# One 4 MB transfer for an expert's input matrix, where there were two of 2 MB

## The chip, the cores and the metric

The kernel runs on one core of one Trainium2 chip. TensorE is written PE, VectorE DVE, ScalarE ACT, GpSimd POOL and SyncE SP. The metric is the device time of one launch in microseconds, as the median of several runs. Before the change it is 3769.35 us (three runs, 3766.24 to 3770.93).

## What is computed

Two networks of two layers each run one behind the other on 512 tokens of width 1024, all in fp32. The first network's layer is a token mixer followed by a mixture of experts; the second's is attention, gating and convolution followed by a dense feed-forward part. The change lies in the mixture of experts of the first network. Cut to that part, the reference is:

```python
def hier_moe(h, w_rg, b_rg, w_re, b_re, w1, w2):       # w1: 32 x 1024 x 1024, w2: 32 x 512 x 1024
    t = h.reshape(-1, d_)                              # 512 tokens
    ...                                                # each token picks a group of 8 experts and 2 experts in it
    order = jnp.argsort(flat_e)
    xs = t[flat_tok[order]]
    hu = lax.ragged_dot(xs, w1, sizes)                 # each expert's tokens by its input matrix
    h_gate, h_up = jnp.split(hu, 2, axis=-1)
    ys = lax.ragged_dot(jax.nn.silu(h_gate) * h_up, w2, sizes)
    ys = ys * flat_gate[order][:, None]
    return jnp.zeros_like(t).at[tok_s].add(ys)

for l in range(DEPTH):                                 # DEPTH = 2
    x = x + g1 * token_mixer(...)
    x = x + g2 * hier_moe(...)
```

An expert's input matrix `w_expert_in[l, e]` is 1024 x 1024 fp32, 4 MB; its output matrix `w_expert_out[l, e]` is 512 x 1024, 2 MB. All 32 experts are read in each layer.

## The kernel before, in words

The program is written out engine by engine, with semaphores between them and no scheduler: each engine runs its own instructions in the order in which they stand, and a waiting instruction holds up all that stands behind it on that engine. Block A (the first network) is a hardware loop over two layers, block B (the second network) another.

**The ring.** All weights go through `ring`, six slots of 2 MB each (128 partitions x 16 KB). In block A's projections slots 0 to 2 and at times 3 to 5 are given to named blocks of weights (`blocks_a`). In the expert phase slots 0, 1, 2 belong to the even experts (u = 0) and 3, 4, 5 to the odd ones (u = 1). An expert's input matrix, cut into rows 0 to 511 and rows 512 to 1023, fills the first two of its slots (j = 0 and j = 1), its output matrix the third (j = 2). Row 128 k + p of a matrix lies in partition p, so each descriptor moves one row of 4 KB.

**SP** issues all weight transfers. `expert` (L581 on) issues those of one expert: for each j it waits until PE has finished with that slot's former contents (`m_in_read[0]`, `m_in_read[1]`, `m_down_made`) and then starts the transfer. The transfers of experts 1 and 0 of a layer are issued ahead of the phase, as soon as the last projections that used those slots are done (`layer_first`); the others come in a loop of pairs. A transfer that SP starts joins one hardware queue, which works the transfers off in order. Behind the last expert of layer 0 SP goes on with the first weights of layer 1 (`w_ada`, then `w_in`, L616), behind the last expert of layer 1 with block B's (`w_in_2`, L645).

**PE** works pair by pair (`pair`, L1219). For an expert it does `gate_up` (input matrix, two runs of 16 matmul instructions of 512 columns, one for each j, with a wait for each slot's landing semaphore), then `turn_x` (transposes of the next expert's tokens), `indices` (which tokens the expert after that takes), and `down` (transposes of the activation, then 16 matmul instructions with the output matrix). The SiLU and the product between `gate_up` and `down` are on ACT (L2245) and DVE (L1816, L1822).

**POOL** gathers an expert's token rows with an indirect transfer (L790) and scatters its results into a scratch tensor (L799). When the last scatter of a layer has landed, POOL loads the results back token by token in four steps (L726, `s_units<-ys_scratch`), DVE adds the two experts' results (L1880), PE turns them (L1237), and DVE adds them to the residual (L1887). Then the next layer, or block B, begins.

Of the kernel before, what the change touches and what calls it, by code (L numbers as in the profile page):

```python
# [35 lines left out]
D = 1024  # L36
# [279 lines left out]
def program(nc, ctx, inp, out):  # L316
    def sb(name, shape, dt=F32):
        return ctx.enter_context(nc.sbuf_tensor("s_" + name, shape, dt))

    def sem(name):  # L320
        return ctx.enter_context(nc.semaphore(name))
# [9 lines left out]
    ring = sb("ring", [P, RING, SLOT])  # L331
# [129 lines left out]
    weights_in_m = [sem(f"m_weights_slot{s}") for s in range(RING)]  # L461
# [73 lines left out]
    def settle(eng):  # L535

        eng.sem_inc(settled, 1)
# [4 lines left out]
    def slot_view(s, k, n):  # L542
        return ring[:, s, 0:k * n].rearrange("p (k n) -> p k n", k=k)
# [14 lines left out]
    def _(sp):  # L558
        def kn(w, c0, n):
            return w.rearrange("(k p) n -> p k n", p=P)[:, :, c0:c0 + n]  # L560
# [6 lines left out]
        def source_a(name, l):  # L567
            kind, j = name[0], name[1] if len(name) > 1 else 0
            if kind == "ada":
                return KD, 512, kn(inp["w_ada"][l], 512 * j, 512)  # L570
            if kind == "lr":
                return KD, 32, kn(inp["w_in"][l], C_LR, 32)
            if kind in ("ya", "yb"):
                return 4, 512, kn(inp["w_branch_a" if kind == "ya" else "w_branch_b"][l], 512 * j, 512)
            if kind == "wo":
                return KD, 512, kn(inp["w_out"][l], 512 * j, 512)
            c = {"gqk": 0, "gv": C_GV, "gg": C_GG, "dq": C_DQ, "dk": C_DK, "dv": C_DV, "ga": C_GA, "gb": C_GB}[kind]
            return KD, 512, kn(inp["w_in"][l], c + 512 * j, 512)
# [3 lines left out]
        def expert(l, number, e, u, layer_first):  # L582

            for j in range(3):
                s = 3 * u + j
                if layer_first:

                    sp.wait_ge(TA.done.sem, TA.done_at(l, RA.reader_last(s) if s < 3 else ("gb", 7)))
                    settle(sp)

                sp.wait_ge(freed_in_m[j].sem, freed_in_m[j].at(number, u - 1))
                settle(sp)
                if j < 2:
                    sp.dma_start(slot_view(s, 4, D), kn(inp["w_expert_in"][l, e], 0, D)[:, 4 * j:4 * j + 4, :]).then_inc(weights_in_m[s], 16)
                else:
                    sp.dma_start(slot_view(s, 4, D), kn(inp["w_expert_out"][l, e], 0, D)).then_inc(weights_in_m[s], 16)

        with sp.Fori(0, DEPTH) as l:
            settle(sp)
            before = sp.value_load(cells[0:1, 0:1], min_val=0, max_val=BLOCKS)  # L600
            for name, *_ in RA.blocks:
                s = RA.slot(name)
                reader = RA.reader_before(name)
                if reader is None:

                    sp.wait_ge(freed_in_m[s % 3].sem, freed_in_m[s % 3].at(before * 2, s // 3 - 1))
                else:
                    sp.wait_ge(TA.done.sem, TA.done_at(l, reader))
                settle(sp)
                if name[0] == "rt":  # L610
                    v = slot_view(s, KD, 36)
                    sp.dma_start(v[:, :, 0:4], kn(inp["w_router_group"][l], 0, 4)).then_inc(weights_in_a[s], 16)
                    sp.dma_start(v[:, :, 4:36], kn(inp["w_router_expert"][l], 0, 32)).then_inc(weights_in_a[s], 16)
                else:
                    k, n, src = source_a(name, l)
                    sp.dma_start(slot_view(s, k, n), src).then_inc(weights_in_a[s], 16)  # L616

            for u in (1, 0):
                expert(l, before * 2, u, u, True)
            sp.wait_ge(routed.sem, routed.at(l, 1))  # L620
            settle(sp)
            ahead = sp.value_load(cells[0:1, 1:2], min_val=NEXP // 2 - 1, max_val=BLOCKS // 2 - 1)

            with sp.Fori(0, ahead) as pair:
                for u in range(2):
                    e = sp.value_load(block_expert[0:1, bass.ds(2 * pair + (2 + u), 1)], min_val=0, max_val=NEXP - 1)
                    expert(l, before * 2 + (2 * pair + 2), e, u, False)

        total = sp.value_load(cells[0:1, 0:1], min_val=0, max_val=BLOCKS)
        with sp.Fori(0, DEPTH) as l:  # L630
            for name, *_ in RB.blocks:
                s = RB.slot(name)
# [9 lines left out]
                j = name[1]  # L642
# [3 lines left out]
                elif name[0] == "up":  # L646
                    i, n = UPS[j]
# [211 lines left out]
    def _(pe):  # L859
        def mm(o, lhsT, rhs, start, stop):  # L860
            return pe.matmul(o, lhsT=lhsT, rhs=rhs, start=start, stop=stop)  # L861
# [37 lines left out]
        with pe.Fori(0, DEPTH) as l:  # L899
# [183 lines left out]
            for i in range(HEADS * NT + 2):  # L1083
# [8 lines left out]
                if i >= 2:  # L1092
                    j = i - 2
# [88 lines left out]
            def gate_up(number, pairs, u):  # L1182

                for j in range(2):
                    s = 3 * u + j
                    pe.wait_ge(weights_in_m[s], pairs * 16 + 16)
                    if j == 0:
                        pe.wait_ge(m_xsT_copied.sem, m_xsT_copied.at(number, u + 1))
                        pe.wait_ge(m_act_made.sem, m_act_made.at(number, u - 1))
                    w = slot_view(s, 4, D)  # L1190
                    for k in range(4):
                        for c in range(2):
                            half = slice(CAP * c, CAP * c + CAP)
                            both = w[:, k, :].rearrange("p (h f) -> p h f", h=2)[:, :, 256 * c:256 * c + 256]
                            last = mm(psum[half, u, :].rearrange("p (h f) -> p h f", h=2), xsT[u][:, k, CAP * j:CAP * j + CAP],
                                      both, j == 0 and k == 0, j == 1 and k == 3)
                    last.then_inc(m_in_read[j].sem, m_in_read[j].more())
# [18 lines left out]
            def pair(number, pairs, e, more_come):  # L1216
                for u in range(2):
                    gate_up(number, pairs, u)
                    if more_come or u == 0:  # L1219
                        turn_x(number, pairs, u + 1)  # L1220
                    if more_come:
                        indices(number, e + (u + 2), u + 2)
                    down(number, pairs, u)
# [17 lines left out]
        with pe.Fori(0, DEPTH) as l:  # L1241
# [117 lines left out]
            for j in range(PAIRS + 3):  # L1359
# [21 lines left out]
                if j in FILL:  # L1381
                    name, a, b = FILL[j]
# [1078 lines left out]
```

## Time and profile before

| | us |
|---|---|
| median of three runs | 3769.35 |
| the profiled execution, its own time | 3768.46 |
| its span in the profile | 3766.8 |
| PE busy | 3173.7 (84% of the span) |
| DVE busy | 1138.5 (30%) |
| ACT busy | 946.6 (25%) |
| POOL busy | 807.7 (21%) |
| moved by DMA | 663.67 MB, of which the SP queue 623.43 MB |

The profile's time starts at the span's start; the 1.66 us between the profiled execution's span and its own time lie outside it. All stretches below are given in microseconds from that start. Layer 0's expert phase is at 679 to 1226 us, layer 1's at 1877 to 2448 us; block B follows. A line such as "PE L861 MATMUL ... x16" sums up 16 instructions that stand next to each other; the figure ahead of it is how long they took together, and the bracket behind it the idle time of that engine ahead of them and what ended it. Matmuls come from one helper (L861), so they are told apart by their operands: `s_ring,s_units 128*64` are those with expert weights. The durations of PE are modelled from records of which a few per cent can be missing.

### The profile page before, as it was taken

The page shows a single profiled execution, that of the slowest core. Times are in us where ns is not written, and L with a number is a line of the kernel's source. Part 1 is how long each engine was busy: PE and PEld are TensorE (multiplying, and loading weights), DVE is VectorE, ACT ScalarE, POOL GpSimd, SP SyncE. Part 2 cuts the span into 40 slices and gives each one's busy share as a digit, 9 for nine tenths or more (in the row PEclk, how much of TensorE's full clock was granted, in tenths as well). Part 3 has the DMA queues.
Part 4 walks back from the last instruction along what each step waited for, and adds up shares of the span by engine and source line. Part 5 has one row for each costly group of instructions (what it writes and reads, how often), then busy time and mean ns, then how long its engine had stood idle before and what let it go on. Part 6 is the DMA issues. An engine that isn't in the chain of part 4 may idle for free. (4 is left out here: it accounts for less than half of the span.)

```text
span 3766.8 us, 42402 instructions
## 1 busy us (share of the span) xinstructions
PE 3173.7 (84%) x15027; PEld 2050.9 (54%) x15027; DVE 1138.5 (30%) x2001; ACT 946.6 (25%) x1337; POOL 807.7 (21%) x382
## 2 busy tenths in 40 slices
PE   6985898788785797699788778597899998889999
PEld 4763564333332575365433323275688776568877
DVE  4555312211111447421311111134243303424330
ACT  4323201111110523211111111133343323334331
POOL 3311010111111222000011111231134343014432
PEclk7997898899997898799799999889899998989999
DMA  5124123799998112413299999810222231022232
GB/s 206 68 77 144 68 90 131 310 408 409 408 407 339 68 68 79 153 54 138 90 396 408 409 409 408 309 57 23 68 83 86 79 118 63 23 68 90 79 88 69
DMA packets 291822, 663.67 MB, mean 176 GB/s; under 512 B 20254, under 2 KB 114772, under 8 KB 291664
## 3 DMA queue, kind: packets, MB, share of 16 engines
q1 hardware_dynamic: 273792, 623.43, 44.6%
q0 software_dynamic: 17872, 38.14, 2.8%
q8 instruction: 98, 1.61, 0.2%
q14 instruction: 60, 0.49, 0.0%
HBM read 653.64 MB, written 25.69 MB: 180 GB/s over the span
## 5 line engine op out<-in xcount | busy, mean ns | idle before, releaser
L861 PE MATMUL psum<-s_parts 128*128 128x512 f32 (+1 forms) x3744 | 951.9, 406 | 84.0 <-ACT s_units L2050 37.7
L861 PEld LDWEIGHTS psum<-s_parts 128*128 128x128 f32 (+1 forms) x3744 | 723.1, 194 | 279.3 <-ACT s_units L2050 46.0
L861 PE MATMUL psum<-s_ring,s_units 128*64 128x512 f32 x3168 | 742.5, 617 | 135.2 <-DMA s_ring<-in_w_expert_in 96.1
L839 POOL TENSOR_TENSOR s_parts<-s_ring,s_parts 128x4096 fp32r<-128x4096 f32 (+2 forms) x52 | 407.9, 7843 | 875.4 <-ACT s_parts L2050 875.4
L861 PEld LDWEIGHTS psum<-s_ring,s_units 128*64 128x64 f32 x3168 | 247.2, 141 | 587.0 <-issue 446.8
L861 PE MATMUL psum<-s_h_low,s_parts 128*128 128x512 f32 (+1 forms) x1872 | 469.8, 391 | 11.2 <-DVE s_hid_low L2021 11.2
L861 PEld LDWEIGHTS psum<-s_h_low,s_parts 128*128 128x128 f32 (+1 forms) x1872 | 350.0, 188 | 95.1 <-DVE s_hid_low L2021 12.1
L861 PE MATMUL psum<-s_units 128*128 (+9 forms) x1520 | 303.6, 420 | 81.8 <-ACT s_units L2050 31.4
L748 POOL TENSOR_TENSOR s_parts<-s_ring,s_parts 128x4096 fp32r<-128x4096 f32 (+1 forms) x22 | 180.5, 8209 | 595.9 <-ACT s_parts L2050 595.9
L2050 ACT ACTIVATE s_parts<-s_ring 128x4096 fp32r<-128x4096 f32 (+3 forms) x74 | 237.3, 3210 | 254.6 <-PE psum L861 103.5
L861 PEld LDWEIGHTS psum<-s_units 64*128 64x128 f32 (+3 forms) x1520 | 177.8, 196 | 163.5 <-issue 109.1
L1810 DVE TENSOR_SCALAR s_put_at<-psum,s_half_row 128x1 int32<-128x1 f32 x66 | 14.4, 218 | 702.9 <-DMA ys_scratch<-s_units,s_put_at 702.9
L861 PE MATMUL psum<-s_units,s_ring 128*128 128x512 f32 x512 | 221.5, 592 | 3.3 <-DVE s_units L1694 3.3
L790 POOL DMA_INDIRECT s_units<-h_scratch,s_take_at x66 | 83.0, 1258 | 594.6 <-DVE s_take_at L1805 474.0
L2050 ACT ACTIVATE s_units<-psum 128x512 f32<-128x512 f32 (+1 forms) x252 | 145.3, 599 | 257.3 <-PE psum L861 210.1
L861 PEld LDWEIGHTS psum<-s_units,s_ring 128*128 128x128 f32 x512 | 97.1, 190 | 123.3 <-issue 122.7
L2030 DVE SCALAR_TENSOR_TENSOR s_units<-psum,s_par,s_units 128x511 f32<-128x511 f32 x88 | 66.0, 750 | 280.8 <-ACT s_units L2413 280.8
L2413 ACT ACTIVATE s_units<-psum,s_par 128x512 f32<-128x512 f32 x88 | 60.7, 690 | 308.7 <-PE psum L861 308.7
L799 POOL DMA_INDIRECT ys_scratch<-s_units,s_put_at x66 | 67.2, 1018 | 322.3 <-ACT s_units L2251 288.0
L2251 ACT ACTIVATE s_units<-psum,s_gsl 128x512 f32<-128x512 f32 x66 | 45.4, 687 | 359.2 <-PE psum L861 359.2
L1504 DVE RECIPROCAL s_temps<-s_temps 128x512 f32<-128x512 f32 x36 | 120.7, 3353 | 25.1 <-ACT s_temps L2075 25.1
L2245 ACT ACT_TABLE_LOAD x31 | 39.8, 1283 | 270.3 <-PE psum L861 270.3
(336 smaller groups left out, 2608.1 us busy)
## 6 DMA issues: line engine op xcount, KB each, us to landing
s_ring<-in_w_expert_in SPq DMA_DIRECT2D x132, 2048.0 KB, 23.9
s_ring<-in_w_expert_out SPq DMA_DIRECT2D x66, 2048.0 KB, 24.8
s_ring<-in_w_in SPq DMA_DIRECT2D x28, 2048.0 KB, 8.0
s_ring<-in_w_ada SPq DMA_DIRECT2D x24, 2048.0 KB, 8.2
s_ring<-in_ffn_w_up SPq DMA_DIRECT2D x40, 1024.0 KB, 6.6
s_ring<-in_ffn_w_down SPq DMA_DIRECT2D x16, 1408.0 KB, 7.0
s_ring<-in_w_out SPq DMA_DIRECT2D x8, 2048.0 KB, 7.8
s_units<-ys_scratch POOLq DMA_DIRECT2D x16, 512.0 KB, 6.0
```

Source lines behind the costliest of these rows:

```text
L748: pool.tensor_tensor(parts[:, s, 0:size], ring[:, s, 0:size], parts[:, 4 + n % 2, 0:size].bitcast(F32), ALU.subtract).then_inc(weights_low ...
L790: pool.indirect_dma_start(out=xs[u % 2], out_offset=None, in_=h2_dram[:, :], in_offset=bass.IndirectOffsetOnAxis(ap=take_at[:, u % 2, 0:1] ...
L799: pool.indirect_dma_start(out=ys_dram[:, :], out_offset=bass.IndirectOffsetOnAxis(ap=put_at[:, u, 0:1], axis=0), in_=ys[u], in_offset=None ...
L839: pool.tensor_tensor(parts[:, s, 0:size], ring[:, s, 0:size], parts[:, 4 + n % 2, 0:size].bitcast(F32), ALU.subtract).then_inc(weights_low ...
L861: return pe.matmul(o, lhsT=lhsT, rhs=rhs, start=start, stop=stop)
L1504: link(ve.reciprocal(T[:, 2, :], T[:, 3, :]))
L1810: ve.tensor_scalar(put_at[:, u % 2, :], psum[:, 7, 1:2], 2.0, half_row[:, 0:1], ALU.mult, ALU.add).then_inc(m_put_written.sem, m_put_writt ...
L2030: link(ve.scalar_tensor_tensor(out=up_t[:, b, 1:SEQ], in0=o[:, 0:SEQ - 1], scalar=w[0], in1=up_t[:, b, 1:SEQ], op0=ALU.mult, op1=ALU.add))
L2050: return ae.activation(o, i, ACT.Copy) if scale is None else ae.activation(o, i, ACT.Copy, scale=scale)
L2245: ae.activation(sil[u], psum[:, u, 0:256], ACT.Silu).then_inc(m_silu_made.sem, m_silu_made.more())
L2251: ae.activation(ys[u], psum[:, 5 + u, :], ACT.Copy, scale=gsl[:, u:u + 1]).then_inc(m_ys_made.sem, m_ys_made.more())
L2413: ae.activation(up_t[:, n % 4, :], o, ACT.Copy, scale=par[:, col:col + 1]).then_inc(up_centre.sem, up_centre.more())
```

## The change

SP no longer starts a transfer at j = 0; it still waits there for `m_in_read[0]`. At j = 1, after the wait for `m_in_read[1]`, it starts one transfer of the whole matrix into the two neighbouring slots, with the same 4 KB rows, and it reports on the first slot's semaphore. PE waits for that semaphore ahead of its first run of `gate_up` and no longer between the two. The output matrix's transfer, the matmuls, and the semaphores by which PE gives slots back are the same.

```diff
                 sp.wait_ge(freed_in_m[j].sem, freed_in_m[j].at(number, u - 1))
                 settle(sp)
-                if j < 2:
-                    sp.dma_start(slot_view(s, 4, D), kn(inp["w_expert_in"][l, e], 0, D)[:, 4 * j:4 * j + 4, :]).then_inc(weights_in_m[s], 16)
-                else:
+                if j == 1:
+                    both = ring[:, s - 1:s + 1, :].rearrange("p a (k n) -> p (a k) n", n=D)
+                    sp.dma_start(both, kn(inp["w_expert_in"][l, e], 0, D)).then_inc(weights_in_m[s - 1], 16)
+                elif j == 2:
                     sp.dma_start(slot_view(s, 4, D), kn(inp["w_expert_out"][l, e], 0, D)).then_inc(weights_in_m[s], 16)
...
                 for j in range(2):
                     s = 3 * u + j
-                    pe.wait_ge(weights_in_m[s], pairs * 16 + 16)
                     if j == 0:
+                        pe.wait_ge(weights_in_m[s], pairs * 16 + 16)
                         pe.wait_ge(m_xsT_copied.sem, m_xsT_copied.at(number, u + 1))
                         pe.wait_ge(m_act_made.sem, m_act_made.at(number, u - 1))
```

SP, in the loop over pairs, the transfers of the even expert of the pair. `m_in_weights_read0` and `1` count PE's two runs of `gate_up`, `m_down_made` counts `down`. Before:

```order
L594 ISA [waits m_in_weights_read0]
L594 DMA s_ring<-in_w_expert_in 128x4x1024
L594 ISA [waits m_in_weights_read1]
L594 DMA s_ring<-in_w_expert_in 128x4x1024
L596 ISA [waits m_down_made]
L596 DMA s_ring<-in_w_expert_out 128x4x1024
```

And now:

```order
L595 ISA [waits m_in_weights_read0,m_in_weights_read1]
L595 DMA s_ring<-in_w_expert_in 128x8x1024
L597 ISA [waits m_down_made]
L597 DMA s_ring<-in_w_expert_out 128x4x1024
```

The first half's transfer has moved behind the wait for the second run, and the two have become one.

PE, in the same loop, `down` of the even expert and `gate_up` of the odd one (slots 3 and 4), which follow each other. The order lists half as many rows as the profile, since each fp32 matmul is issued as two instructions. Before:

```order
L861 MATMUL psum<-s_ring,s_units 64x512 [waits m_ys,m_actT,m_weights_slot2]
L861 MATMUL psum<-s_ring,s_units 64x512 x7
L861 MATMUL psum<-s_ring,s_units 64x512 [waits m_act,m_xsT_copied,m_weights_slot3]
L861 MATMUL psum<-s_ring,s_units 64x512 x7
L861 MATMUL psum<-s_ring,s_units 64x512 [waits m_weights_slot4]
```

And now:

```order
L862 MATMUL psum<-s_ring,s_units 64x512 [waits m_ys,m_actT,m_weights_slot2]
L862 MATMUL psum<-s_ring,s_units 64x512 x7
L862 MATMUL psum<-s_ring,s_units 64x512 [waits m_act,m_xsT_copied,m_weights_slot3]
L862 MATMUL psum<-s_ring,s_units 64x512 x15
```

The wait between the two runs of `gate_up` is gone, and the one ahead of them is for the whole matrix.

## Rows read from the trace of the kernel before

**Rows 1.** The page: span, then tenths busy and rates in 40 slices.
```profile
span 3766.8 us, 42402 instructions
...
DMA  5124123799998112413299999810222231022232
GB/s 206 68 77 144 68 90 131 310 408 409 408 407 339 68 68 79 153 54 138 90 396 408 409 409 408 309 57 23 68 83 86 79 118 63 23 68 90 79 88 69
```
**Rows 2.** Stretches of the expert phases: busy per engine, then PEclk, DMA share, GB/s.
```profile
700.00:1160.00 460.00, 380.25 (x1806) 153.49 (x1804) 55.47 (x175) 64.83 (x101) 66.29 (x58) 0.97 1.03 407
1885.00:2400.00 515.00, 425.18 (x2024) 171.42 (x2022) 61.94 (x193) 73.84 (x115) 74.29 (x65) 0.97 1.02 407
...
1165.00:1178.00 13.00, 9.17 (x42) 2.61 (x38) 0.61 (x2) 1.07 (x2) 1.01 (x1) 1.00 0.80 308
```
**Rows 3.** Line L594 for issues at 685, 688, 702, 718, 1060 to 1160.
```profile
DMA to landing us min/median/max: 8.2/8.2/8.2
...
DMA to landing us min/median/max: 10.9/10.9/10.9
...
DMA to landing us min/median/max: 14.2/14.2/14.2
...
DMA to landing us min/median/max: 13.7/13.7/13.7
...
DMA to landing us min/median/max: 23.1/25.0/27.8
```
**Rows 4.** Timeline, both phases' starts: start us, us, what.
```profile
678.88 9.13 PE L861 MATMUL psum<-s_ring,s_units 128*64 128x512 f32 x32 [0.84 <-ACT s_units L2050]
685.25 3.39 SPq L594 DMA_DIRECT2D s_ring<-in_w_expert_in  x2
...
1883.02 3.62 SPq L594 DMA_DIRECT2D s_ring<-in_w_expert_in  x2
```
**Rows 5.** Timeline of PE in layer 0, the last three experts, all `gate_up` and `down`.
```profile
1146.86 3.65 PE L861 MATMUL psum<-s_ring,s_units 128*64 128x512 f32 x16 [0.56 <-DMA s_ring<-in_w_expert_out]
1151.78 3.65 PE L861 MATMUL psum<-s_ring,s_units 128*64 128x512 f32 x16 [1.26 <-DMA s_ring<-in_w_expert_in]
1157.02 3.65 PE L861 MATMUL psum<-s_ring,s_units 128*64 128x512 f32 x16 [1.58 <-DMA s_ring<-in_w_expert_in]
...
1162.77 3.65 PE L861 MATMUL psum<-s_ring,s_units 128*64 128x512 f32 x16 [0.56 <-DMA s_ring<-in_w_expert_out]
1167.76 3.65 PE L861 MATMUL psum<-s_ring,s_units 128*64 128x512 f32 x16 [1.33 <-DMA s_ring<-in_w_expert_in]
1172.74 3.65 PE L861 MATMUL psum<-s_ring,s_units 128*64 128x512 f32 x16 [1.33 <-DMA s_ring<-in_w_expert_in]
...
1178.34 3.65 PE L861 MATMUL psum<-s_ring,s_units 128*64 128x512 f32 x16 [0.56 <-DMA s_ring<-in_w_expert_out]
```
**Rows 6.** Timeline of PE in layer 1: one slower run, and the last expert.
```profile
2355.09 5.35 PE L861 MATMUL psum<-s_ring,s_units 128*64 128x512 f32 x16 [2.25 <-DMA s_ring<-in_w_expert_in]
...
2402.66 3.65 PE L861 MATMUL psum<-s_ring,s_units 128*64 128x512 f32 x16 [1.46 <-DMA s_ring<-in_w_expert_in]
...
2408.26 3.65 PE L861 MATMUL psum<-s_ring,s_units 128*64 128x512 f32 x16 [0.56 <-DMA s_ring<-in_w_expert_out]
```
**Rows 7.** Timeline of SP: the transfers ahead of the phase, and behind its end.
```profile
593.66 27.86 SPq L594 DMA_DIRECT2D s_ring<-in_w_expert_in  x2
...
1171.67 13.38 SPq L616 DMA_DIRECT2D s_ring<-in_w_ada  x4
```
**Rows 8.** Timeline behind layer 0's last `down`: the scatter, the loads, the last addition.
```profile
1183.78 0.98 POOL L799 DMA_INDIRECT ys_scratch<-s_units,s_put_at  x1 [14.48 <-ACT s_units L2251]
1191.06 2.21 POOL L726 DMA_DIRECT2D s_units<-ys_scratch  x4 [6.30 <-issue]
...
1216.32 1.23 DVE L1880 TENSOR_TENSOR s_units<-s_units 128x1024 f32<-128x1024 f32 x1 [2.82 <-DMA s_units<-ys_scratch]
```
**Rows 9.** The same places in layer 1: first load, last addition.
```profile
2419.67 2.20 POOL L726 DMA_DIRECT2D s_units<-ys_scratch  x4 [4.97 <-issue]
...
2438.14 1.22 DVE L1880 TENSOR_TENSOR s_units<-s_units 128x1024 f32<-128x1024 f32 x1 [1.78 <-DMA s_units<-ys_scratch]
```

## The prediction

> **What bounds the kernel now.** I began with the page's 40 slices [rows 1]. In slices 8 to 12 and 21 to 25 the DMA digit is 9 nearly throughout and the rate 396 to 409 GB/s; everywhere else the core moves 23 to 206 GB/s for the most part. Those are the two expert phases, and the change touches nothing outside them. The table of stretches [rows 2] shows them apart: 407 GB/s and a DMA share of 1.03 and 1.02, while PE is busy 380 of 460 us and 425 of 515 us. So the phases are bound by the transfers, and PE has some idle time in each expert.
>
> Then I asked how deep the queue is, since this decides whether a later start of a transfer matters. The time from SP's issue to landing [rows 3] is 8.2 us at the phase's start, 13.7 to 14.2 us two experts later, and 25 us (23.1 at least) in the last hundred microseconds. 2 MB at 409 GB/s take 5.13 us, so late in the phase a transfer has more than three others ahead of it. The reader should see that slots come back faster than the queue delivers: PE gives them back early, and they wait in the queue.
>
> Last, the timeline at both ends. At the start [rows 4] all six slots are full, the queue is empty, and SP's first transfer of the loop goes out at 685.25, when PE has read the first half. At the end [rows 5] PE waits for each landing: half 0 at 1167.76, half 1 at 1172.74, output matrix at 1178.34.
>
> **The steady part.** Removed: one transfer and one wait of PE per expert. Moved: the first half's transfer, to the moment of the second's. What hides it is the queue. The second half is issued at the same place as the 4 MB transfer will be, and it lands 23.1 us later at least [rows 3]; the data of 4 MB take 10.3 us, 10.9 with the gathers beside them. That leaves over 12 us of other transfers ahead. The cover is thinnest right after the start. The second half issued at 702 lands after 14.2 us, the one issued at 718 after 13.7; less 10.9 us of data that is 3.3 and 2.8 us, against about 3.1 us from an issue to its data on an empty queue (8.2 less 5.13). Since the whole queue is by then 3 us late (next part), the margin is near 3 us in both. So I expect no gap in the queue, and cost: 0.
>
> PE starts `gate_up` only when both halves are there. In the queue's order that is when half 1 landed before, so PE runs 3.65 us late into the next step. Its chain per expert at full clock is 7.30 (two runs of 3.65), then 2.1 to 2.2 us from the end of `gate_up` to `down` (1157.02 + 3.65 = 1160.67 to 1162.77 [rows 5]), then 3.65 for `down`: 13.1 us against a period of 1167.76 - 1151.78 = 15.98 us. The idle time, now in two pieces of 1.3 to 1.6 us, becomes one of about 2.9 us. Cost while PE is the one that waits: 0.
>
> Does one transfer in place of two make the stream itself faster? No row shows a 4 MB transfer. A bound from rows: at the end, with no gather beside it, half 1 is picked up 1172.74 - 1167.76 = 4.98 us after half 0 [rows 5], no longer than its 5.13 us of data. Nothing is left between the transfers to be saved; I allow 0.1 us either way for each of the 64 pairs of transfers that come behind a full queue, so 6 us up or down, and take 1 us off in all, near the row's nothing, since there are half as many completions.
>
> By the Trainium skill ("DMA: Bandwidth & Descriptors", "Anatomy of one DMA") a transfer costs some 2.0 us fixed plus its bytes. Were that paid in a full queue, 66 fewer transfers would be an estimated 130 us off, and the forecast some 3650 us. This trace disagrees: a 2 us gap behind each 5.13 us of data would give 7.1 us between landings, and the row has 4.98. The page's own rules say that the fixed part overlaps where a transfer is issued early.
>
> **The start of each phase.** The queue is empty and the phase is bound by it, so the first issue sets when the stream begins. Layer 0: SP's two issues begin at 685.25 and, the pair of them taking 3.39 us and one 0.37, at 688.27 [rows 4]. The 4 MB transfer goes out at 688.27: 3.0 us late. Layer 1: 1883.02 + 3.62 - 0.37 = 1886.27, so 3.25 us late. A stream that is always busy never makes this up. Together +6.3 us. Were the queue not bound after all in some stretch, part would be regained; 0 is the lower end, and 6.3 what I take.
>
> The transfers ahead of the phase change as well: half 0 of expert 0, issued at 593.66, goes with half 1 at 621 [rows 7]. It then lands some 13 us later, and PE wants it at 678.88. Cost 0.
>
> **The end of each phase.** For the last expert nothing hides the later `gate_up`: it starts at 1172.74 and has 7.30 us to do where 3.65 were left, and activation, `down` and scatter follow in a chain. +3.65 us. In layer 1 the same from 2402.66 [rows 6]. Together +7.3 us. If the 2.9 us of idle time ahead lets the clock fall, the run that took 5.35 us in place of 3.65 behind a wait of 2.25 us [rows 6] gives the price: +1.7 each. I take 0.5 each, +1.0.
>
> Against this stands a relief. Behind the last expert SP's weights for the next stage share the queues with the loads of the results. In layer 0 it takes 1217.5 - 1191.06 = 26.5 us from the first of these loads to the last addition [rows 8], in layer 1, where fewer weights are fetched, 2439.4 - 2419.67 = 19.7 us [rows 9]. The difference, 6.8 us, is what the w_ada and w_in transfers cost. They are held by the queue, which is 3 us late, more than by PE, which is 6.7 us late; so they come some 3.6 us earlier relative to the loads. Of about 20 us of sharing that is a sixth, which would save 1.2 us in layer 0; in layer 1 less, say 0.8. Relief -2.0 us; bounds 0 and -7.2 (all the extra lateness of PE hidden in both layers).
>
> **The sum.** +6.3 + 7.3 + 1.0 - 2.0 = +12.6 us, less the 1 us for the completions: +11.6 us. From the profiled execution's own 3768.46 us that is 3780.1; it lies 0.9 us under the median of 3769.35, so the forecast for the median is 3781.0 us.
>
> **The rivals.**
>
> A. The tail is hidden: the loads of results wait for the weights of the next stage anyway, and only the late start counts: +6.3 us, 3775.6. For it: the scatter issued at 1183.78 is followed by loads only at 1191.06 [rows 8], in a busy queue. Against it: in layer 1 the loads run mostly free of such company and would show the whole 3.65 us. Chance 0.16.
>
> B. The other side: the stream gets faster. Each pair of transfers becomes one with a single set of completions, and the place is the full queue between 700 and 1160 us and its twin. It decides the result if it saves more than 0.3 us per pair: 64 x 0.3 = 19.2, which turns +11.6 into -7.6 us, 3761.7. For it: the share falls to 0.80 in 1165 to 1178 us [rows 2] while the last transfers are still under way, so the DMA engines don't finish together, and how they share out work might depend on the size. Against it: the 4.98 us above. Chance 0.05.
>
> C. PE becomes the bound. One idle piece of 2.9 us per expert could drop the clock each time, once ahead of `gate_up` and once ahead of `down`. Two stretches at half clock at 1.7 us make the chain 13.1 + 3.4 = 16.5 us against 15.98: 0.5 us over in each of some 55 experts, so +28 us beside the +11.6, 3809 us. For it: the run of 5.35 us [rows 6] went in part at 1.2 GHz, behind a wait of 2.25 us. Against it: the clock granted over the phases is 0.97 of the full one [rows 2] with such waits in it, and as soon as PE is late the idle piece is gone. Chance 0.06.
>
> The Trainium skill ("TensorE: Matmul & The Clock Gate", "Loop structure matters more than you think") warns of just this form, a long wait for a transfer ahead of each burst of matmuls, and would have every expert start cold. By that rule C is the outcome. The rows bear it out in part only, hence its chance.
>
> D. The queue runs dry, because a transfer twice as long is issued later or SP is stopped until there is room for it. It costs up to the 2 to 3 us of margin per expert for the first few experts, +5 to +10 us beyond the forecast: 3789. Chance 0.03.
>
> **How the numbers follow.** Forecast 0.70, A 0.16, B 0.05, C 0.06, D 0.03. A measurement of this kernel can tell about 0.2%, 7.5 us, from no change. The forecast's own spread is about 4 us around +11.6 (the tail's terms, and half of the 6 us for the stream), so about a sixth of it falls under +7.5. Slower: 0.58 of the forecast's 0.70, 0.05 of A's 0.16, all of C and D: 0.72. Same: the other 0.12 of the forecast, 0.11 of A, 0.01 of B: 0.24. Faster: 0.04 of B. The range leaves out C and most of B: 3772 to 3789 us.
>
> **What would show it.** In the profile after: the expert input as x66 of 4096 KB; the loop's first issue at 688.3 and near 1889; 407 to 409 GB/s as before within the phases; PE rows of x32 with 7.3 us and one wait ahead of each; the issue to landing of the 4 MB transfers near 25 us late in the phase. Layer 0's last `down` would end 6.7 us late, near 1188.7, and its last addition end near 1223. A landing period other than 16 us per expert would break the steady part, a PEclk well under 0.95 would speak for C, a GB/s figure under 400 in the first 100 us for D, and a difference of 3 us per layer in place of 6 for A.

## The result, and the profile after

The changed kernel takes 3780.14 us (median of 7 runs, 3772.55 to 3782.89) against 3769.35 us before (7 runs, 3762.2 to 3771.14). The ratio is 1.0031, 95% interval 1.0021 to 1.0041: slower by 11.7 us, 7.9 to 15.5 (the medians are 10.8 us apart). The forecast was 3781.0 us, 11.6 us above before.

Lines of the page after, answering to [rows 1], and two of its DMA issues (count, KB each, median us from issue to landing):

```profile
span 3774.6 us, 42204 instructions
...
GB/s 206 67 77 144 67 94 135 308 409 409 407 408 327 68 68 77 151 53 143 90 384 408 409 409 407 319 57 23 67 68 101 73 107 79 23 68 90 78 88 69
...
s_ring<-in_w_expert_in SPq DMA_DIRECT2D x66, 4096.0 KB, 24.5
s_ring<-in_w_expert_out SPq DMA_DIRECT2D x66, 2048.0 KB, 22.5
```

In the middle of both phases the rate is what it was, 407 to 409 GB/s. At their edges it has changed, for instance 327 for 339 in slice 13 and 384 for 396 in slice 21 (counted from 1). The stretches of the kernel after, with the columns of [rows 2], agree:

```profile
700.00:1160.00 460.00, 381.20 (x1781) 153.33 (x1781) 55.14 (x173) 64.53 (x101) 66.91 (x58) 0.95 1.02 408
1885.00:2400.00 515.00, 428.07 (x2001) 173.11 (x1999) 62.05 (x194) 72.16 (x112) 73.78 (x64) 0.95 1.01 401
1165.00:1178.00 13.00, 9.72 (x38) 3.23 (x40) 0.42 (x1) 0.87 (x2) 1.00 (x1) 0.87 0.49 199
```

The count x66 is not 2 x 32. Layer 0 fetches 32 input matrices and layer 1 fetches 34, since an expert with more than 64 tokens takes two turns and its weights are read twice. So layer 1's phase is the longer one, and 62 of the 66 turns are in the loops over pairs.

The 401 of the second line isn't a slower stream: the stretch opens at 1885 us, and the first transfer of that phase is issued at 1891.04 where it was 1883.02, 8 us or 1.6% of the stretch. The third line is the tail of layer 0, where the share has fallen from 0.80 to 0.49.

The timeline after, at the start of both phases, answers to [rows 4] (start us, us, what; the line numbers are one higher):

```profile
676.74 9.13 PE L862 MATMUL psum<-s_ring,s_units 128*64 128x512 f32 x32 [0.84 <-ACT s_units L2051]
686.23 0.38 SPq L595 DMA_DIRECT2D s_ring<-in_w_expert_in  x1
...
1881.48 9.21 PE L862 MATMUL psum<-s_ring,s_units 128*64 128x512 f32 x32 [0.84 <-ACT s_units L2051]
...
1891.04 0.38 SPq L595 DMA_DIRECT2D s_ring<-in_w_expert_in  x1
```

The first issue comes 9.49 us after PE's first `gate_up` where it was 6.37 us (before, the second issue came at 9.39). Everything else has to be read from that first `gate_up` too, since the phases start at other absolute times in each execution (676.74 for 678.88, 1881.48 for 1876.8). Issue and landing times below are read in the same way.

The timeline after at the end of layer 0's phase, answering to [rows 5] and [rows 8], and the last expert of layer 1, answering to [rows 6]:

```profile
1156.79 7.09 PE L862 MATMUL psum<-s_ring,s_units 128*64 128x512 f32 x32 [2.69 <-DMA s_ring<-in_w_expert_in]
...
1165.98 3.65 PE L862 MATMUL psum<-s_ring,s_units 128*64 128x512 f32 x16 [0.56 <-issue]
1172.35 8.78 PE L862 MATMUL psum<-s_ring,s_units 128*64 128x512 f32 x32 [2.71 <-DMA s_ring<-in_w_expert_in]
...
1183.08 3.65 PE L862 MATMUL psum<-s_ring,s_units 128*64 128x512 f32 x16 [0.56 <-issue]
...
1188.52 0.98 POOL L800 DMA_INDIRECT ys_scratch<-s_units,s_put_at  x1 [16.02 <-ACT s_units L2252]
1195.06 2.20 POOL L727 DMA_DIRECT2D s_units<-ys_scratch  x4 [5.55 <-issue]
...
1219.78 1.23 DVE L1881 TENSOR_TENSOR s_units<-s_units 128x1024 f32<-128x1024 f32 x1 [2.18 <-DMA s_units<-ys_scratch]
...
2410.34 7.09 PE L862 MATMUL psum<-s_ring,s_units 128*64 128x512 f32 x32 [1.05 <-DMA s_ring<-in_w_expert_in]
...
2419.37 3.65 PE L862 MATMUL psum<-s_ring,s_units 128*64 128x512 f32 x16 [0.56 <-issue]
...
2448.47 1.23 DVE L1881 TENSOR_TENSOR s_units<-s_units 128x1024 f32<-128x1024 f32 x1 [2.15 <-DMA s_units<-ys_scratch]
```

Two runs of 3.65 us with a wait each have become one of 7.09 with one wait ahead, of 2.7 us in layer 0 and 1.05 us at layer 1's last expert. The form is as foretold. The last run of layer 0 takes 8.78 us: it begins at the lower of the two clock levels (granted clock 0.54 in 1172.3 to 1176 us, 1.00 behind that), the 1.2 GHz one. I call this a cold start below.

Measured from each phase's first `gate_up`, in us (start of the first run, SP's first issue in the loop, end of the last `down`, end of the last addition L1880 or L1881), of this pair and of the kernels below that keep the same structure:

```
                     first issue      last down ends    last addition ends   both     rest of
                     L0      L1       L0       L1        L0       L1         phases   the span
before               6.37    6.22     503.11   535.11    538.67   562.56     1101.2   2665.6
after                9.49    9.56     509.99   541.54    544.27   568.22     1112.5   2662.1
e1_sp_late           9.76    9.66     505.07   538.36    540.20   565.89     1106.1   2664.2
e2_pe_both           6.35    6.19     506.22   540.35    540.65   566.57     1107.2   2660.6
e3_two_late          9.31    9.65     508.33   546.97    542.36   570.46     1112.8   2662.7
e4_one_again         9.43    9.57     509.79   541.36    544.07   567.80     1111.9   2668.8
e5_quarters          4.00    3.99     498.29   532.07    533.62   561.42     1095.0   2666.4
e6_in_quarters       3.99    3.99     500.79   535.51    535.84   562.73     1098.6   2665.2
```

The phases are 11.3 us longer, 5.6 in layer 0 and 5.7 in layer 1. The rest of the span, in which the change touches nothing, differs by up to 8 us between executions (2660.6 to 2668.8) and hides part of this in a single profile: the spans are only 7.8 us apart. The phases scatter less. The three programs that were profiled twice agree in their sum to 0.3 to 0.6 us (after 1112.5 and e4_one_again 1111.9 among them). The kernel before has one profile only, and every difference of phases here is against that one.

### The profile page after: what moved, and what is told of

The parts are those of the page before. It is cut to its first block and busy times, and to the rows that moved or that the text cites. A ratio compares the mean times of both kernels' runs of the same rounds, so it can differ in the third digit from the quotient of the medians.

```text
span 3774.6 us, 42204 instructions
## 1 busy us (share of the span) xinstructions
PE 3185.2 (84%) x15027; PEld 2055.1 (54%) x15027; DVE 1138.4 (30%) x2001; ACT 946.2 (25%) x1337; POOL 809.0 (21%) x382
## 5 line engine op out<-in xcount | busy, mean ns | idle before, releaser
L862 PE MATMUL psum<-s_ring,s_units 128*64 128x512 f32 x3168 | 757.3, 632 | 131.1 <-DMA s_ring<-in_w_expert_in 92.3
L1811 DVE TENSOR_SCALAR s_put_at<-psum,s_half_row 128x1 int32<-128x1 f32 x66 | 14.4, 218 | 707.9 <-DMA ys_scratch<-s_units,s_put_at 707.9
## 6 DMA issues: line engine op xcount, KB each, us to landing
s_ring<-in_w_expert_in SPq DMA_DIRECT2D x66, 4096.0 KB, 24.5
```

## The experiments

My theory from here on I call the ends theory. The stream of transfers binds and isn't touched. The cost is a first issue that comes about 3 us later in each phase, and a last `gate_up` that begins only when all is there. Against it stand the size theory (a 4 MB transfer is itself the worse, or the better, one), the hidden tail (rival A) and PE as the bound (rival C).

**Each part by itself.** In e1_sp_late only SP's part is changed, and the transfers stay two:

```diff
-                if j < 2:
-                    sp.dma_start(slot_view(s, 4, D), kn(inp["w_expert_in"][l, e], 0, D)[:, 4 * j:4 * j + 4, :]).then_inc(weights_in_m[s], 16)
-                else:
+                if j == 1:
+                    for h in range(2):
+                        sp.dma_start(slot_view(s - 1 + h, 4, D), kn(inp["w_expert_in"][l, e], 0, D)[:, 4 * h:4 * h + 4, :]).then_inc(weights_in_m[s - 1 + h], 16)
+                elif j == 2:
```

> Two transfers of 2 MB as before, but SP issues both only behind the wait for the second run of gate_up; PE still waits for each half by itself. Ends theory (the cost is a later first issue per phase and a later last gate_up per phase): only the start's part remains, +2 to +3 us in each phase, so +4 to +6 us over before; nothing at the tail. Size theory (the cost comes from one transfer of 4 MB in place of two): 0 us. Hidden-tail theory (only the start counts, rival A of the prediction): the whole difference of the changed kernel, +11 us, or near it.

Measured: ratio 1.0018 (1.0007 to 1.0028), +6.8 us; the phases 4.9 us longer, 1.5 and 3.3. The end of layer 0's phase keeps its form, two runs with a wait each:

```profile
1170.09 3.65 PE L862 MATMUL psum<-s_ring,s_units 128*64 128x512 f32 x16 [1.09 <-DMA s_ring<-in_w_expert_in]
1175.07 3.65 PE L862 MATMUL psum<-s_ring,s_units 128*64 128x512 f32 x16 [1.33 <-DMA s_ring<-in_w_expert_in]
1180.67 3.66 PE L862 MATMUL psum<-s_ring,s_units 128*64 128x512 f32 x16 [0.56 <-DMA s_ring<-in_w_expert_out]
```

The size theory's 0 lies outside the interval of 2.6 to 10.6 us. The hidden tail's 11 does so only narrowly, but the phases, 4.9 us longer where the changed kernel's are 11.3, speak against it too. The late start costs something by itself, but not all.

In e2_pe_both only PE's part is changed:

```diff
-                    pe.wait_ge(weights_in_m[s], pairs * 16 + 16)
                     if j == 0:
+                        for h in range(2):
+                            pe.wait_ge(weights_in_m[s + h], pairs * 16 + 16)
```

> SP as before, two transfers of 2 MB issued each behind its own wait; PE waits for both halves ahead of gate_up. Ends theory: only the tail's part, 3.65 us per phase plus up to 1.7 us where the clock has fallen, less a us or so of relief in the loads behind: +5 to +8 us over before, gate_up rows of x32 in the steady part, the first issue as early as before. Size theory: 0 us. Hidden-tail theory: 0 us. PE-bound theory (rival C): +20 us or more.

Measured: ratio 1.0020 (1.0011 to 1.0029), +7.5 us; the phases 6.0 us longer, 2.0 and 4.0, with the first issue where it was before. Layer 1's last expert here begins at the lower clock, layer 0's doesn't:

```profile
1170.12 7.09 PE L861 MATMUL psum<-s_ring,s_units 128*64 128x512 f32 x32 [2.96 <-issue]
...
2403.92 8.78 PE L861 MATMUL psum<-s_ring,s_units 128*64 128x512 f32 x32 [2.82 <-issue]
```

That is most of the 2 us by which the two layers differ. The hidden tail asked for 0 and PE as the bound for 20 us or more; the interval is 4.1 to 10.9 us. So the tail isn't hidden (rival A), and PE isn't the bound (rival C).

**Both parts, and the size alone.** e3_two_late has both edits; it differs from the changed kernel only in moving the matrix as two transfers.

> Both of the above: two transfers of 2 MB, both issued behind the second wait, and PE waits for both. It differs from the changed kernel in the size of the transfer alone. Ends theory: +10 to +13 us over before, the same as the changed kernel within 2 us. Size theory: 0 us, and the changed kernel 11 us above it. If one transfer on an empty queue lands sooner than two of half the size, as the first one of the phase seems to (13.2 us from issue to landing for 4 MB, against 14.0 and 14.6 for the two before), this kernel is 1 to 2 us slower than the changed one.

> The changed kernel again, beside the others on the same chip: +11 us over before (ratio 1.003), between 8 and 15.

Measured on the same chip: e3_two_late 1.0038 (1.0024 to 1.0051), +14.3 us; e4_one_again, the changed kernel once more, 1.0030 (1.0019 to 1.0040), +11.3 us. Their phases are 11.6 and 10.6 us longer than before, and 4.9 + 6.0 = 10.9 is the sum of the two parts. So the parts add up to the whole. One transfer for two is worth nothing that can be told: the medians of the two kernels are 0.5 us apart (3780.24 and 3779.74), and the ratios 3 us, with intervals that overlap. The landing of the first matrix of the phase shows it too; from SP's first issue (line L595 of each kernel, issue to landing, one transfer of 4 MB in e4_one_again, two of 2 MB in e3_two_late):

```profile
DMA to landing us min/median/max: 13.2/13.2/13.2
```

```profile
DMA to landing us min/median/max: 7.7/10.3/12.9
```

These are layer 0's. The two of e3_two_late are issued 0.6 us apart, so its second half is there 13.5 us after the first issue, against 13.2 us. In layer 1 it is 14.4 against 13.0 us. In e1_sp_late, which issues in the same way as e3_two_late, both layers take 13.2 us, so this too doesn't show a cost of the size.

By layers the phases of e3_two_late are 1.7 us shorter than those of e4_one_again in layer 0 and 2.7 us longer in layer 1, and neither points at the size. In layer 0 the last `gate_up` runs at full clock (7.09 us for 8.78). At the end of layer 1 several cold starts come one behind the other. Each row of x48 is a `down` and the `gate_up` behind it, 10.5 us in most of the phase:

```profile
2389.40 13.29 PE L862 MATMUL psum<-s_ring,s_units 128*64 128x512 f32 x48 [0.56 <-issue]
...
2407.06 12.99 PE L862 MATMUL psum<-s_ring,s_units 128*64 128x512 f32 x48 [0.56 <-issue]
```

The granted clock is 0.50 in 2389 to 2393 and again in 2407 to 2411 us, and no wait for weights stands ahead of `gate_up` in these rows. Here PE itself is the one that is late, and `down` ends 5.4 us later than in the changed kernel. That is rival C on a small scale.

**The other way.** If the ends cost what I say, smaller pieces must give it back. In e5_quarters each slot is filled by two transfers of 1 MB, each with a landing semaphore and a read count of its own, for both matrices; in e6_in_quarters for the input matrix alone. The core of e5_quarters:

```diff
+                for q, (gate, landed) in enumerate(((m_early_read[j], weights_in_m[s]), (freed_in_m[j], weights_in_q[s]))):
+                    sp.wait_ge(gate.sem, gate.at(number, u - 1))
+                    settle(sp)
+                    src = kn(inp["w_expert_in"][l, e], 0, D)[:, 4 * j + 2 * q:4 * j + 2 * q + 2, :] if j < 2 else kn(inp["w_expert_out"][l, e], 0, D)[:, 2 * q:2 * q + 2, :]
+                    sp.dma_start(slot_view(s, 4, D)[:, 2 * q:2 * q + 2, :], src).then_inc(landed, 16)
...
                     for k in range(4):
+                        if k == 2:
+                            last.then_inc(m_early_read[j].sem, m_early_read[j].more())
+                            pe.wait_ge(weights_in_q[s], pairs * 16 + 16)
```

> The kernel before with every transfer of expert weights cut the other way: each 2 MB slot is filled by two transfers of 1 MB (8 k-rows become 4 pairs), SP starts each as soon as PE has read its part, PE waits for each part by itself, input and output matrix alike. Ends theory: the opposite sign of the change. First issue about 3 us earlier in each phase, last gate_up part 1.8 us instead of 3.65 and down ending about 2 us earlier: -4 to -5 us per phase, -6 to -10 us under before. Size theory (larger transfers are better for the stream, smaller ones worse; or the change's cost lies in the size): slower than before, or the same.

> The same, but for the input matrix alone; the output matrix stays one transfer of 2 MB. Ends theory: the start's gain is kept, -2 to -3 us per phase; at the tail gate_up ends 1.8 us earlier, but down then waits for the output matrix, which lands when down begins now, so nearly nothing: -4 to -6 us under before in all. Size theory: the same as before or slower.

Measured: e5_quarters 0.9995 (0.9984 to 1.0005), e6_in_quarters 0.9988 (0.9978 to 0.9997), or -1.9 and -4.5 us. So e5_quarters missed the -6 to -10 us that I had said, by its times. The profiles are clearer: first issue 2.2 to 2.4 us earlier, phases 6.2 and 2.7 us shorter than before. The end of layer 0's phase in e5_quarters has runs of x8, where [rows 5] had x16, and `down` begins 3.88 us after the last of them, where it was 5.60 us:

```profile
1164.21 1.94 PE L862 MATMUL psum<-s_ring,s_units 128*64 128x512 f32 x8 [0.56 <-DMA s_ring<-in_w_expert_in]
1167.07 1.94 PE L862 MATMUL psum<-s_ring,s_units 128*64 128x512 f32 x8 [0.93 <-DMA s_ring<-in_w_expert_in]
1170.95 3.65 PE L862 MATMUL psum<-s_ring,s_units 128*64 128x512 f32 x16 [0.56 <-issue]
```

In e6_in_quarters the last `down` waits 1.90 us for the output matrix, which is why the tail gives back less there:

```profile
1176.53 3.65 PE L866 MATMUL psum<-s_ring,s_units 128*64 128x512 f32 x16 [1.90 <-DMA s_ring<-in_w_expert_out]
```

Both once more, with their expectations:

> The quarters once more, since their first ratio (0.9995) and their profile (phases 6 us shorter than before) disagree in size. Ends theory: -4 to -7 us, ratio 0.998 to 0.999. If cutting costs the stream something (twice as many transfers), 0 or above.

> The input matrix alone in quarters once more. Ends theory: -2 to -4 us by its phases (2.7 us shorter), so its first ratio of 0.9988 (-4.5 us) was a little lucky; below before, ratio 0.999.

Measured: 0.9992 (0.9983 to 1.0001) and 0.9995 (0.9986 to 1.0004), phases 6.7 and 2.9 us shorter than before. In us the times are -3.0, where I had said -4 to -7, and -1.9. All four ratios are under 1, by 2 to 5 us, yet three of the four intervals hold 1. In the phases of the profiles the sign has turned, as the ends theory asks. Why the times of e5_quarters and e9_quarters_again show only a third to a half of what the phases do stays open. That the kernel as a whole gains is likely and not shown; by the four ratios it is about 0.1%.

**How much room PE has.** e7_extra2 and e8_extra6 are the changed kernel with 2 and 6 more matmuls behind each `down` in the loop; their results go to an unused bank:

```diff
                     down(number, pairs, u)
+                    if more_come:
+                        for x in range(2):
+                            mm(psum[:, 3, :], ident[:], hT[:, x, :], True, True)
```

> The changed kernel with 2 more matmuls (128x512 fp32, 0.85 us each at full clock, into an unused PSUM bank, their result is not used) behind each down inside the loop over pairs: 1.7 us more PE work per expert. Slack theory (the stream binds, PE idles 2.7 to 3.7 us ahead of each gate_up): within 3 us of the changed kernel, with fewer half-clock stretches. PE-bound theory (rival C: the idle piece and the clock make PE the bound): +1.7 us in each of 60 experts, +100 us.

> The same with 6 more matmuls, 5.1 us per expert, more than the idle piece. Slack theory: PE becomes the bound by 5.1 less about 3 us of slack, some 2 us in each of 60 experts, +90 to +150 us over the changed kernel, and GB/s under 409 in the phases. PE-bound theory: 5.1 us in each, +300 us.

Measured: e7_extra2 1.0031 (1.0021 to 1.0040), the changed kernel's own ratio, with some 1.8 us more of PE work in each expert; its PEclk in 700 to 1160 us is 0.98, above the 0.95 of the changed kernel. e8_extra6 takes 3944.1 us, ratio 1.0463 (1.0448 to 1.0478), 164 us above the changed kernel. I had said 90 to 150. Two stretches of it, one in each phase, and the six matmuls (`s_hT,s_ident`) with the `gate_up` behind them:

```profile
700.00:1160.00 460.00, 434.87 (x1824) 176.47 (x1822) 48.84 (x150) 55.11 (x86) 57.52 (x49) 1.00 0.90 348
1985.00:2500.00 515.00, 487.81 (x2043) 197.74 (x2042) 53.03 (x164) 61.47 (x95) 63.10 (x54) 1.00 0.90 349
...
1237.08 5.42 PE L862 MATMUL psum<-s_hT,s_ident 128*128 128x512 f32 x12
1242.43 7.09 PE L862 MATMUL psum<-s_ring,s_units 128*64 128x512 f32 x32
```

The rate is 348 and 349 GB/s where it was 407 and more, and `gate_up` follows without a wait: now PE binds. The six matmuls put `gate_up` off by 5.35 us (0.89 us each). Over the 62 turns of the two loops 164 us are 2.65 us each, so some 2.7 us of the 5.35 were free. The chain of PE in the changed kernel has that much room, and one cold start takes 1.7 us of it. One cold start per expert fits into it, two don't.

## Why the prediction was right

Term by term, from the first `gate_up` of each phase, layer 0 and layer 1:

- **The steady part, forecast 0.** 407 to 409 GB/s in the middle slices after as before, and 24.5 us from issue to landing in the median. (The prediction counts slice 8 to the busy ones; its rate is 310 GB/s before, and the full rate holds in slices 9 to 12 and 22 to 25. Nothing rests on this.) The figure of the Trainium skill that the prediction sets against its 4.98 us ("DMA: Bandwidth & Descriptors", "Anatomy of one DMA") is the page's fit for transfers that POOL issues, while the weights here are issued by SP. So the trace disagrees with the use that was made of it, and not with the page. The cover held: between the first landing of a phase and its last the lateness changed by -0.8 us in layer 0 and +1.2 us in layer 1. The last matrix is picked up at 1172.35 - 676.74 = 495.61 us against 1172.74 - 678.88 = 493.86, so +1.75, and in layer 1 at 528.86 against 525.86, so +3.0.
- **The start, forecast +6.3.** The issue came late as computed, by 3.1 and 3.3 us. What reached the end of the stream is 4.75 us (1.75 and 3.0, the line above). So the term was 1.5 us too large, or 0.5 with the 1 us that the sum takes off for fewer completions. The other kernels with the late issue give the same against the profile of before: 1.6 and 2.8 us in e4_one_again, 1.95 and 3.3 us in e1_sp_late. Measured at the first full landing of the phase, the lateness against the profile of before is 2.5 and 1.8 us: there the second half landed 13.9 us after layer 0's first issue (3.0 + 10.9 [rows 3]) and 14.6 us after layer 1's, while after the change the 4 MB are there in 13.3 and 13.1 us. The issues to landing of the kernel after, for the two of 685 to 700 us and the one at 1891 us:

```profile
DMA to landing us min/median/max: 13.3/14.7/16.0
...
DMA to landing us min/median/max: 13.1/13.1/13.1
```

  A quick reading would be that two transfers issued 3 us apart land late as such. e2_pe_both, which issues as the kernel before does, shows a scatter there: 13.3 and 13.5 us to the second landing for 13.9 and 14.6. What both early kernels share lies a little later. From 16 to 26 us after the first `gate_up` of layer 0, with the columns of [rows 2], in the kernel before, e2_pe_both, the kernel after and e1_sp_late:

```profile
694.90:704.90 10.00, 8.11 (x44) 3.46 (x40) 0.61 (x3) 1.67 (x3) 1.03 (x1) 1.00 0.99 380
692.60:702.60 10.00, 7.50 (x38) 2.86 (x33) 0.00 (x0) 1.67 (x3) 1.03 (x1) 1.00 0.99 356
692.70:702.70 10.00, 8.81 (x48) 4.03 (x44) 0.76 (x4) 1.67 (x3) 1.03 (x1) 1.00 1.02 410
695.30:705.30 10.00, 8.53 (x46) 3.91 (x43) 0.61 (x3) 1.67 (x3) 1.03 (x1) 1.00 1.02 406
```

  In layer 1 it is 376 and 383 GB/s against 411 and 408, and e3_two_late and e4_one_again, late as well, have 404 to 410 in both layers. So where the first transfer goes out early, the stream then runs some 7 to 13% under its full rate for about 10 us. 100 us after the first `gate_up` the kernel before is ahead of the one after by bytes worth 1.8 us in layer 0 and 2.2 us in layer 1, 4.0 us in all, where its issues were 6.4 us earlier. The term took the whole lead to survive; this is the step that it had wrong.

  What fits is the third transfer. It is the output matrix, its slot comes back with `down`, and it is issued at 16.4 to 16.7 us in the kernels before and after alike. In the kernel before, the first two land by 20.3 and 20.8 us, so their data are nearly through when the third's begin. The rate is lowest just there, 324 and 295 GB/s in the two microseconds from 18 to 20 us in layer 0, 273 and 274 in layer 1. After the change the 4 MB last to 22.6 us and more, and those microseconds have 406 to 418 GB/s. No run moves the third issue by itself, so this is argued and not shown.

  The 1 us for fewer completions isn't shown either: e3_two_late and e4_one_again, which would show it, differ by their cold starts.
- **The tail, forecast +7.3 and +1.0 for the clock.** From the last landing to the end of `down` +5.13 in layer 0 (8.78 for 3.65) and +3.43 in layer 1 (7.09 for 3.65), 8.6 in all. One of the two last experts began at the lower clock, at the price of 1.7 us that a run of before had shown. The half of a chance for each was a guess, and that exactly one of two came is partly luck. Over the five kernels with one wait per expert in which the stream binds (after, e2 to e4, e7) it came in 6 of 10; in e7_extra2 it came in both layers (8.54 and 8.60 us).
- **The relief, forecast -2.0.** From the end of `down` to the last addition it is 34.28 us for 35.56 and 26.68 for 27.45: -1.28 and -0.77, so -2.05. The size is right and the reason isn't. I had the w_ada transfers come 3.6 us earlier relative to PE. They come later, since it is PE that holds them, not the queue: PE gives slot 3 back only behind the first half of the last `gate_up`. They are issued at 1171.67 before and at 1177.96 after,

```profile
1177.96 10.07 SPq L617 DMA_DIRECT2D s_ring<-in_w_ada  x4
```

  which is 492.8 and 501.2 us after the first `gate_up`: 8.4 us later where the scatter is 6.9 us later. The DMA share of 0.49 in 1165 to 1178 us, where it was 0.80, fits with the hole that this leaves. Scatter and first loads then went a little faster (6.54 us from the scatter to the loads for 7.28 [rows 8]). That this is from less traffic beside them fits, but no run isolates it.

The sum of the measured terms is 4.75 + 8.6 - 2.05 = 11.3 us, the forecast's was 11.6. That it comes this close is in part luck: single terms were off by up to 1.5 us and scatter by as much.

Of the rivals, A is refuted by e2_pe_both and B by e3_two_late beside e4_one_again, which differ by far less than the 19 us that it needs. D didn't happen: from 16 to 100 us after the first `gate_up` the rate after is 406 to 411 GB/s in both layers. C happened in its first half only: the granted clock did fall from 0.97 to 0.95 [rows 2] with the longer idle piece. In the changed kernel this had no effect in mid-phase that can be seen, since a cold start costs 1.7 us out of room that e8_extra6 measures as some 2.7 us; it did have one where several came together, in layer 1 of e3_two_late. The Trainium skill's warning on waits ahead of bursts of matmuls ("TensorE: Matmul & The Clock Gate", "Loop structure matters more than you think") is borne out in part. Of the 40 `gate_up` rows of x32 in the timeline after, 13 took 8.5 us or more and 27 took 7.09 us, so about one in three started cold and not each. In the changed kernel the price was paid at the last expert of layer 0, where no idle time of PE was left to take it up. Nor would a cold start in each expert by itself have led to C, as the prediction says: that needs two per expert.

## What to carry to other kernels

Where a full queue of transfers binds a stretch, as here, the size and the issue time of one transfer in its middle cost nothing as long as the queue stays covered and the computing engine keeps some idle time. What counts is the stretch's ends: how soon the first slot comes back once the stretch begins, and how much work is left when the last byte lands. Add up both ends once for each time the stretch is entered; don't multiply by the number of transfers. A head start at the first issue counts in full only if the next transfers are issued early enough to keep the queue filled behind it. A cost that is small against the scatter of whole runs is best read from marks inside the trace, taken from a common start.

## What I had not expected

- An early first issue gains less than its lead. The two kernels that issue 3 us earlier (before and e2_pe_both) run at 356 to 383 GB/s from 16 to 26 us after the first `gate_up`, the four with the late issue (after, e1, e3, e4) at 404 to 411.
- The same issues on an empty queue land at times that differ by about a microsecond. Two transfers of 2 MB issued 3 us apart land 13.9 and 14.6 us after the first issue in the kernel before, 13.3 and 13.5 us in e2_pe_both. Two issued 0.6 us apart take 13.2 us in both layers of e1_sp_late, 13.5 and 14.4 us in e3_two_late. One of 4 MB takes 13.0 to 13.3 us in its four cases.
- More work made PE's clock better: with 1.8 us of added matmuls per expert PEclk rose from 0.95 to 0.98, and the ratio stayed. Of the 62 `gate_up` rows of x32 in its timeline only 3 took 8.5 us or more. Two of these were the last of the phases, where they count, and its phases are 2.8 us longer than the changed kernel's.
